# A DeltaNet scan whose chunk inverse is built transposed

## The reference, cut to what matters

```python
decay = where(causal, exp(g[..., :, None] - g[..., None, :]), 0)   # g: cumulative sums in the chunk
lmat = where(strict, einsum('bhnid,bhnjd->bhnij', kb, k) * decay, 0)   # kb = k * beta
a = lmat + eye(64)
u = triangular_solve(a, v * beta)          # lower, unit diagonal
w = triangular_solve(a, kb * exp(g))
attn = einsum('bhnid,bhnjd->bhnij', q, k) * decay
# then, chunk after chunk, with a 64x64 state per head and direction:
v_new = u - w @ state
o = (q * exp(g)) @ state + attn @ v_new
state = state * exp(g_last) + (k * exp(g_last - g)).T @ v_new
```

## Time and profile before

| | us |
|---|---|
| median of 3 runs (1802.16 to 1807.4) | 1805.83 |
| the profiled execution | 1807.76 |
| its span, first to last instruction | 1806.0 |

### The profile page before, as it was taken

One profiled execution on the slowest core, in us unless ns is written; L12 is line 12 of the kernel. 1 busy time (PEld: TensorE's weight loads), 2 busy tenths in 40 slices (PEclk: granted clock), 3 DMA queues, 4 the chain that ended last, 5 costly groups with the idle time before them and its releaser, 6 DMA issues. The chain is left out here.

```text
span 1806.0 us, 35848 instructions
## 1 busy us (share of the span) xinstructions
PE 1484.5 (82%) x15686; PEld 1247.8 (69%) x15686; DVE 800.7 (44%) x1233; ACT 606.5 (34%) x984; POOL 258.2 (14%) x233
## 2 busy tenths in 40 slices
PE   6599999966998967778399963799999999999940
PEld 1499999854786256668245540789998999889940
DVE  0511343153554345554323352545556464554625
ACT  2611211054666233322211110445344443444411
POOL 0400000001441043324700004100000000000012
PEclk9699999987999979999699966899999999999975
DMA  8210010017453510000142245466656666566436
GB/s 314 76 44 24 24 40 32 30 30 163 142 173 123 177 33 4 5 4 5 37 181 70 81 146 135 152 211 243 219 204 253 212 231 230 202 245 218 177 128 233
DMA packets 124721, 237.16 MB, mean 131 GB/s; under 512 B 30578, under 2 KB 48754, under 8 KB 124562
## 3 DMA queue, kind: packets, MB, share of 16 engines
q1 hardware_dynamic: 110164, 184.50, 31.7%
q0 software_dynamic: 9792, 33.57, 5.0%
q10 hardware_dynamic: 4608, 16.78, 2.3%
HBM read 196.34 MB, written 34.28 MB: 128 GB/s over the span
## 5 line engine op out<-in xcount | busy, mean ns | idle before, releaser
L2311 PE MATMUL psum<-hgT_high,unit_high 128*128 128x256 f32 x1024 | 290.5, 284 | 2.0 <-ACT hgT_high L2221 2.0
L2312 PE MATMUL psum<-hgT_low,unit_high 128*128 128x256 f32 x1024 | 290.5, 284 | 0.0
L2313 PE MATMUL psum<-hgT_high,unit_low 128*128 128x256 f32 x1024 | 290.4, 284 | 0.0
L2266 DVE TENSOR_TENSOR unit_low<-arena,unit_high 128x2048 fp32r<-128x2048 f32 x96 | 214.3, 2287 | 78.9 <-ACT unit_high L2215 78.9
L2215 ACT CAST unit_high<-arena 128x2048 fp32r<-128x2048 f32 x96 | 177.3, 1917 | 68.3 <-PEq L2638 57.7
L2311 PEld LDWEIGHTS psum<-hgT_high,unit_high 128*128 128x128 f32 x1024 | 197.2, 193 | 3.0 <-ACT hgT_high L2221 2.4
L2312 PEld LDWEIGHTS psum<-hgT_low,unit_high 128*128 128x128 f32 x1024 | 197.3, 193 | 0.6
L2313 PEld LDWEIGHTS psum<-hgT_high,unit_low 128*128 128x128 f32 x1024 | 197.3, 193 | 0.0
L588 PE MATMUL psum<-w_high,hT_high 128*128 128x256 f32 (+3 forms) x504 | 143.2, 284 | 11.7 <-DVE w_low L545 11.7
L588 PE MATMUL psum<-w_high,hT_low 128*128 128x256 f32 (+3 forms) x504 | 143.5, 285 | 0.0
L588 PE MATMUL psum<-w_low,hT_high 128*128 128x256 f32 (+3 forms) x504 | 143.3, 284 | 0.0
(11 more groups left out here) (283 smaller groups left out, 2782.5 us busy)
## 6 DMA issues: line engine op xcount, KB each, us to landing
arena<-in_w_gate SPq DMA_DIRECT2D x32, 1024.0 KB, 9.4
arena<-in_w_up SPq DMA_DIRECT2D x32, 1024.0 KB, 5.4
arena<-in_w_down SPq DMA_DIRECT2D x32, 1024.0 KB, 8.1
arena<-in_w_ada SPq DMA_DIRECT2D x12, 2048.0 KB, 10.8
slot_rows<-arena ACTq DMA_DIRECT2D x32, 512.0 KB, 4.5
arena<-in_rpb_table SPq DMA_DIRECT2D x192, 48.0 KB, 2.0
arena<-in_x_sample SPq DMA_DIRECT2D x16, 512.0 KB, 11.9
w_whole<-in_w_in SPq DMA_DIRECT2D x8, 1024.0 KB, 5.4
```

Of the source, the lines that this page charges most:

```text
L2266: nc.vector.tensor_tensor(s.unit_low[j % UNIT_X], s.unit_x[j % UNIT_X], s.unit_high[j % UNIT_H].bitcast(F32), ALU.subtract).then_inc(low_d ...
L2311: nc.tensor.matmul(out, w[0], x[0], start=first, stop=False)
L2312: nc.tensor.matmul(out, w[0], x[1], start=False, stop=False)
L2313: return nc.tensor.matmul(out, w[1], x[0], start=False, stop=last)
```

## The change

The scan builds the inverse of the transposed matrix. The products of a level then have `L` itself as their first factor, so `lower_turned`, its copy `LT` and the final `inverse_turned` go; what is still turned in each level, `X`, goes through four whole-array transposes into a PSUM bank of the lane's own (`turns`, banks 4 and 6) instead of 16 products into the lane's banks. The products now pick the bank by chunk or head, and `masked` is one instruction. `X` starts from the gram and a mask `B0` that GpSimd makes, beside `BM`; the last `improved` becomes `solved`, which writes `ZF`. The sums of g are spread by one product with the block matrix, its right factor made by GpSimd in `BM` (`sums`). `keys` writes `Y`, so it waits for the lane's last correction, and stands at the end of the round, in round 4 behind the last `step_rows` and ahead of `windows`. The state's update `DS` shares a bank with `V`, and `values` stands right before `state_products` and waits for the state. One constant of 128 columns is added (`swap`), with one product and one ScalarE copy in `stage_dn_prepare`.

```diff
+            def sums(lane, k):
+                if k >= 1: pool.wait_ge(l_ready[lane], k)
+                nc.gpsimd.tensor_tensor(blocks(s.BM[lane]), over_heads(s.tri64), spread_cols(s.g, t), ALU.mult).then_inc(sums_ready[lane], 1)
             def decayed_masks(lane, k):
+                pool.wait_ge(spread[lane], k + 1)
+                nc.gpsimd.tensor_tensor(blocks(s.BM[lane]), over_heads(s.strict64), spread_cols(s.beta, t), ALU.mult)...
+                nc.gpsimd.tensor_tensor(blocks(s.B0[lane]), over_heads(s.level64[:, 0]), spread_cols(s.beta_pair, t), ALU.mult)...
                 pool.wait_ge(e_ready[lane], k + 1)
+                nc.gpsimd.tensor_tensor(s.B0[lane], s.B0[lane], s.E[lane], ALU.mult).then_inc(b0_ready[lane], 1)
                 nc.gpsimd.tensor_tensor(s.BM[lane], s.BM[lane], s.E[lane], ALU.mult)...
                 ...
             def keys(lane, k):
-                    pool.wait_ge(w_done[lane], 4 * k)
+                pool.wait_ge(zy_done[lane], 4 * LEVELS * (k + 1))
...
             def turned_out(lane, k, m):
-                act.wait_ge(y_ready[lane], LEVELS * k + m)
-                nc.scalar.copy(s.Z[lane]..., both[lane][:, :, 256:512])
+                act.wait_ge(z_turned[lane], LEVELS * k + m)
+                nc.scalar.copy(s.Z[lane], turns[lane]).then_inc(z_ready[lane], 1)
...
             for k in range(ROUNDS):                                   # VectorE
                 for lane in here:
+                    first_inverse(lane, k)
                     lower(lane, k)
                     attention(lane, k)
-                for lane in here:
-                    first_inverse(lane, k)
...
             def spread_sums(lane, k):
-                for b in range(8):
-                    for c in chunks:
-                        mm = nc.tensor.matmul(staging[rows(c), ...], g, s.tri64[rows(c), b // 4], ...)
+                nc.tensor.matmul(turns[lane], s.block, s.BM[lane], start=True, stop=True).then_inc(spread[lane], 1)
...
+            def inverse_turned(lane, k, m):
+                ...
+                for e in range(4):
+                    tr = nc.tensor.transpose(turns[lane][:, e * P:(e + 1) * P], s.X[lane][:, e * P:(e + 1) * P], s.ident)
+                tr.then_inc(z_turned[lane], 1)
...
                 for m in range(1, LEVELS + 1):                        # TensorE
                     for lane in here:
                         level_products(lane, k, m)
+                        inverse_turned(lane, k, m)
+                    if m <= 2 and has(m - 1, k + 1):
+                        pe.wait_ge(z_ready[m - 1], LEVELS * k + m)
+                        keys_turned(m - 1, k + 1)
                     if 1 <= k < 4 and m in (3, 4):
+                        values(2 * (k - 1) + m - 3)
                         state_products(2 * (k - 1) + m - 3)
...
                     for lane in here:
                         corrections(lane, k, m)
+                    if m <= 2 and has(m - 1, k + 1):
+                        spread_sums(m - 1, k + 1)
...
-                for lane in here:
-                    inverse_turned(lane, k)
                 for lane in here:
                     keys_solved(lane, k)
```

More of the change, by code:

```diff
@@ L1101, in _ @@
                     late_rows(t // 4)
+            pe.wait_ge(sig_done, 1)
+            nc.tensor.matmul(s.bank[5][:, 0:NT * G2], s.swap, s.beta, start=True, stop=True).then_inc(paired, 1)
             pe.wait_ge(g_done, 1)
@@ L1281, in _ @@
             for lane in (0, 1):
-                beta_masks(lane, 0)
+                sums(lane, 0)
+            for lane in (0, 1):
                 decayed_masks(lane, 0)
@@ L1285, in _ @@
                 for lane in (0, 1):
-                    if has(lane, k):
-                        keys(lane, k)
+                    if has(lane, k + 1):
+                        sums(lane, k + 1)
                 if k < 4:
@@ L1291, in _ @@
                     if has(lane, k + 1):
-                        beta_masks(lane, k + 1)
                         decayed_masks(lane, k + 1)
-            for p in range(4, len(STEPS)):
-                step_rows(p)
+                if k == 4:
+                    for p in range(4, len(STEPS)):
+                        step_rows(p)
+                for lane in (0, 1):
+                    if has(lane, k):
+                        keys(lane, k)
             windows(0)
@@ L1304, in keys_out @@
                     act.wait_ge(gram[lane], 4 * k)
-                nc.scalar.copy(s.qkT[lane], staging).then_inc(qk_ready[lane], 1)
+                nc.scalar.copy(s.qkT[lane], turns[lane]).then_inc(qk_ready[lane], 1)
             def decay(lane, k):
@@ L1432, in first_inverse @@
             def first_inverse(lane, k):
-                dve.wait_ge(l_half[lane], k + 1)
-                dve.wait_ge(l_ready[lane], k + 1)
-                nc.vector.tensor_tensor(blocks(s.X[lane]), blocks(s.L[lane]), over_heads(s.level64[:, 0]), ALU.mult).then_inc(x_half[lane], 1)
+                dve.wait_ge(b0_ready[lane], k + 1)
+                dve.wait_ge(gram[lane], 4 * (k + 1))
+                for odd in (0, 1):
+                    ins = nc.vector.tensor_tensor(head_pairs(s.X[lane], odd), products(lane, odd, 1), head_pairs(s.B0[lane], odd), ALU.mult)
+                ins.then_inc(x_half[lane], 1)
                 dve.wait_ge(x_half[lane], k + 1)
@@ L1440, in masked @@
                 dve.wait_ge(lx_done[lane], 4 * (LEVELS * k + m))
-                if m == 1:
-                    dve.wait_ge(l_turned[lane], 4 * (k + 1))
-                ps = both[lane][:, :, 0:256].rearrange("p d (h j) -> p d h j", h=4)
-                for r in dirs:
-                    ins = nc.vector.tensor_tensor(blocks(s.L[lane])[:, r], ps[:, r], s.level64[:, m, r].unsqueeze(1).to_broadcast([P, 4, HEAD]), ALU.mult)
-                ins.then_inc(y_ready[lane], 1)
+                if m == 1 and k >= 1:
+                    dve.wait_ge(w_done[lane], 4 * k)
@@ L1512, in _ @@
                     for lane in here:
-                        improved(lane, k, m)
+                        if m < LEVELS:
+                            improved(lane, k, m)
+                        else:
+                            solved(lane, k)
+                    if m <= 2 and has(m - 1, k + 1):
+                        differences(m - 1, k + 1)
                     if 1 <= k < 4 and m in (3, 4):
@@ L1616, in keys_solved @@
                 pe.wait_ge(kg_ready[lane], k + 1)
-                kg = blocks(s.kg[lane])
+                kg = blocks(s.Y[lane])
                 for h in range(4):
@@ L1721, in _ @@
                     grams(lane, k)
-                for lane in here:
-                    lower_turned(lane, k)
                 for m in range(1, LEVELS + 1):
@@ L2517, in constants @@
         "other": ~same,
+        "swap": (i[:, None] ^ 1) == i[None, :],
         "before": i[:, None] < i[None, :],
```

231 lines of the change are left out of this document (99 added, 132 removed).

## The result

The changed kernel takes 1784.84 us in the median of four runs (1782.98 to 1784.93), beside 1806.62 for the kernel before on the same chip: a ratio of 0.9882, 95% interval 0.9864 to 0.99. The profiled execution has a span of 1782.9 us, against 1806.0.

The account below looks back on a forecast made before the run. Levels were taken as bound by a dependency chain and TensorE's instruction supply. Gains 1.3 + 8.7 + 34.1 + 6.1 less 5.9 made 44.3; less 5.5 (supply) and 8 (clock), 30.8, so 1775 us, range 1760 to 1793.

Parts of the forecast that it names:

- The two corrections: Taken off the summed gain of 44.3 us: 5.5 for TensorE's instruction supply and 8 for its clock, leaving 30.8.
- The pauses were supply: TensorE's weight loads pause every some 253 instructions, 68 a us at most; 20.6 us of such idle time in the levels.
- the first rival: The pauses are not supply: their 20.6 us stay, the chain alone shortens, gain 15.7, 1790 us; chance 0.13.
- The copy released early: In each level the turned inverse's copy, 0.58 us, runs beside `masked` instead of waiting for it, done at 1.8 us.
- Seams: Between rounds, last `solved` to next `masked`: 8.6 us with two lanes, 6.5 of it VectorE's; 6.4 with one lane.
- A plain level: Level without other work: one lane's chain from products to `improved` 3.45 us, the level entered at 3.6 in round 0.
- Round 4: Last round, one lane: 6.4 + 4 x 7.0 + 3.8 = 38.2 us against 44.3, levels at 464 instructions by 68 a us.
- Levels 3 and 4: In rounds 1 to 3 TensorE sets the time: lanes 2.8 and five state groups 2.3, so 5.0 us each.
- the supply correction: m = 3 to 5 ask 84 instructions a us, 68 come: 1.5 us a round, 1 in round 0, 5.5 in all.
- clock, four seams: TensorE almost idle at each seam, clock falls, calls of 32 cost 0.88 for 0.47: 2 us each, 8 (0 to 16).
- the second rival: GpSimd gates the seam: `keys` comes 4 us late in four rounds, 16 us, gain 15, 1790 us; chance 0.10.
- the third rival: TensorE stays at half clock since transposes replace products: at 60% of its work 20 us slower, 1826 us; chance 0.07.

Follow-up runs that it names:

- the kernel with the pauses: Changed kernel with round 4's `values` put back ahead of the wait for the state, its products in two banks; 1784.1 us, ratio 0.9903.
- the pair without: Changed kernel with `windows` spread over the rounds, 1763.73 us, and the same with round 4's `values` also put back ahead of their wait, 1759.71 us.
- the filler of transposes: Changed kernel plus transposes nobody reads, behind the grams from round 1 on and behind lane a's first transposes in rounds 1 to 3; 1778.77 us, ratio 0.9864.

## Why the prediction was right, and where it was off

It forecast 1775 in a range of 1760 to 1793; the time is 1784.84. The direction and the mechanism hold, and the gain is 21.8 us by the medians where 30.8 were forecast. These are its own steps, before any correction, beside the profiled execution. A seam goes from the last `solved` to the next `masked`, a level from lane a's `masked` to the next, and round 4 to its last corrections:

| step | forecast | trace |
|---|---|---|
| up to the first `masked` | 1.3 gained | 1.4 |
| round 0 | 21.7 | 24.6 |
| rounds 1 to 3: seam, each | 8.6 | 7.7, 7.7, 7.9 |
| level 1, each | 4.7 | 7.0, 7.0, 6.6 |
| level 2, each | 5.8 | 6.1, 6.1, 4.2 |
| levels 3 and 4 together, each round | 10.0 | 12.0, 13.3, 13.3 |
| level 5, each | 3.6 | 4.8, 4.3, 4.3 |
| round 4 | 38.2 | 43.6 |
| later start of `windows` | 5.9 lost | 5.9 |
| clock, four seams | 8 lost | 6.0 in the levels behind them |

The steps up to round 4 come out 22.2 us over the forecast in all. The two corrections had set 13.5 us down against that, partly for causes other than those that the runs show, so some of the nearness of the number is luck.

**The pauses were supply: right.** Their time went from 20.6 to 1.8 us on the level's TensorE lines, and they came back when instructions were added at equal TensorE time, again some 250 instructions apart. So the first rival (the pauses stay) did not happen. Nor does the Trainium skill's "Instruction fetch mechanics" (in "Runtime: NRT & Kernel Launch"), by which crossing a block of instructions is mostly hidden, hold here: 602 instructions a round cost 3.1 us a round. In m = 3 to 5 of rounds 1 to 3 four pauses over 0.35 us are left, 0.39, 0.47, 0.65 and 0.82, together 2.3, for the 4.5 that I set down.

**The copy released early: right, and small.** 2.6 us by the traces of the experiment that takes it back.

**Seams: right, and shorter than set.** They gave 11.9 of the 28.0 us in front of `windows`; that it is `lower_turned`, `inverse_turned` and their copies which are missing there is argued from the two traces, no run put those steps back. In rounds 1 to 3 they take 0.7 to 0.9 less than the 8.6 set down. The forecast took 0.99 us for the identity, or 1.42 beside a GpSimd instruction; but in the trace GpSimd works beside both of these rows. In these seams of the changed kernel five of six run without it, in 0.69:

```profile
681.09 0.69 DVE L1437 TENSOR_TENSOR arena<-arena 128x512 f32<-128x512 f32 x1
```

**A plain level: 4.0 for 3.6.** (The terms set down for it add up to 3.34, not to the 3.45 written.) At m = 4 of round 0 lane a's copy is done at 670.87, and its `corrections` begin at 671.38, since lane b's products and transposes stand ahead of them in TensorE's queue:

```profile
670.28 0.59 ACT L1339 COPY arena<-psum 128x512 f32<-128x512 f32 x1 [1.01 <-PE psum L1600]
...
671.38 0.56 PEld L1613 LDWEIGHTS psum<-arena 64*64 64x64 f32 x32 [0.17 <-issue]
```

**Round 4, the term that was mis-sized: 0.7 us gained for 6.1.** I set its level at 464 instructions by 68 a us, 7.0 us. But it isn't bound by supply: 60 instructions more at equal TensorE time changed nothing there. A level still takes 7.76, as the 7.5 to 8.2 before. These are lane a's `masked` of two levels in the timeline:

```profile
805.86 0.68 DVE L1444 TENSOR_TENSOR arena<-psum,arena 128x512 f32<-128x512 f32 x1
...
813.62 0.68 DVE L1444 TENSOR_TENSOR arena<-psum,arena 128x512 f32<-128x512 f32 x1
```

What sets the pace is TensorE's queue in order (7.5 of 7.8 us busy) with two steps of the state in each level, each of them a chain through ScalarE and VectorE. In that chain the change put `values` between the wait for `s_ready` and `state_products`. I had that at nothing, on the ground that it takes the place of other products; it doesn't, since `state_products` now waits for TensorE's own `values`, seen in the weight loads of round 4:

```profile
810.68 0.54 PEld L1670 LDWEIGHTS psum<-arena 64*64 64x64 f32 x16 [0.23 <-PE psum L1648]
```

In all such waits make 4.4 us, 18 times in the scan. Putting `values` back gave 0.3 us of a level in the kernel with the pauses and 0.6 in the pair without, and there 2.9 us of the round. So this explains about half of the 5.4 that are missing. Another 1.4 is the clock: with the filler of transposes the first level takes 7.96 for 9.34. The rest, some 1.1 us, is open: the forecast had no chain for this round, only a rate.

**Levels 3 and 4: 38.5 us in three rounds for 30.0.** TensorE sets the time there as said: it is busy 6.00 of the 6.09 us of m = 3 in round 1. But the groups don't follow each other at 0.46. From `values` to `state_products` is 0.77 us and from products to transposes 0.76 (at 704.02), twice a wait of 0.17 comes before a group. Those make 1 us a level, 6 of the 8.5 too many, and three of the pauses above make 1.9. In the forecast 4.5 of the 8.5 stood in the supply correction, which so covered a cause beside its own.

**Level 1: the clock at the place named and by the price named.** I set 8 us, between 0 and 16, from calls of 32 products at half clock. The filler of transposes gave 1.9, 1.8, 0.9 and, in round 4, 1.4: 6.0. The same 64 corrections of the earlier trace rows show both levels again, at m = 1 and m = 2 of round 1:

```profile
688.89 1.99 PE L1613 MATMUL psum<-arena 64*64 64x64 f32 x64
...
695.88 1.16 PE L1613 MATMUL psum<-arena 64*64 64x64 f32 x64
```

Round 0 has it too, and there I had set nothing: its m = 1 takes 6.2 us at 0.73, behind a stretch in which TensorE was busy 9.4 of 19.3 us. At the 4.7 us set down for it, that is half of the 2.9 by which round 0 was off; no run filled that stretch, so that the clock is the cause there is not shown.

**Level 5** was 0.7 to 1.2 longer in each round: the queries go there in rounds 1 to 3 too, 0.47 us that I had left out, and one of the pauses.

**GpSimd at the seam (the second rival)** did not decide: `keys_solved` waits for `keys` 4.7 us in eight times, 0.9 at most, in which my 0.9 for lane b is already. But its mechanism is real: with three instructions of `windows` ahead of the `keys` of round 2, the seam grew by the 0.9 us that `keys` was late.

**TensorE at half clock throughout (the third rival)** did not come about. The clock is 0.91 in rounds 1 to 3, lost at the end of the seam (0.89) and in level 1 (0.63), and what loses it is not that transposes stand in for products: 32 transposes more cure it. (The forecast counted 20 transposes a round before; the trace has 12 in round 2.)

**`windows`** came out at the 5.9 us forecast. The prediction took its place as given; the greatest single time of the scan, 26 us of one engine alone, stood in it.

**Of the signs** that were named, the copy into `Z` released by TensorE and `windows` behind the last corrections came; rounds of 33 to 37 us came in one of three (37.6, 38.3 and 36.2), the 8 to 10 us behind `solved` were 7.7 to 7.9, and the scan ended at 870 for 860. Of the signs of being wrong one came once: ahead of round 0, lane b's first inverse waited 1.0 us for GpSimd.

## What to carry to other kernels

Where TensorE's weight loads pause without a semaphore at even distances, count instructions and not busy time; but apply such a rate only where the pauses are, since a level that TensorE's own time and its waits fill, as in round 4, keeps its pace when its instructions are cut. Work taken off TensorE may be given back as clock just behind the stretch that got thin, so the granted clock of the next level belongs in the sum. And look at what ends a stage: here moving eleven of GpSimd's last fourteen instructions under the rounds, without saving one, was worth some 20 us, nearly as much as the whole change.

## What the runs showed of the hardware that was not expected

A wait of TensorE for its own last group, without any other engine, costs some 0.24 us between two groups (4.4 us, 18 times). Sixteen transposes at the end of a seam and sixteen in level 1 held the granted clock at 1.00, where without them it fell to 0.63 over the level. A product ahead of a level's own is paid in full: with the single product added, TensorE was busy 5.8 us more in round 0, and the round took 5.7 us longer; a filler behind the grams, where TensorE waits for VectorE, made the seam no longer (7.7 us). And the branch over a stage that doesn't run, the same in all kernels, took TensorE 0.38 us in eight of them and 3.4 to 3.7 in three.
